# Sliding-window and chunked attention inside a two-block kernel: the division by the softmax sums moves from GpSimd to ScalarE, and two steps of VectorE move with it

## The chip, the cores and the metric

The kernel runs on one core of a Trainium2 chip. The metric is the device time in microseconds of one execution. Three executions of the kernel before took 1228.63, 1229.01 and 1231.67 us; the median is 1229.01 us.

## The reference

Two transformer blocks in fp32, one after the other, over 512 tokens of width 1024. The first block has a projection, sliding-window attention with sinks, a gated convolution, a merge, and a feed-forward part; the second is two layers, each with chunked attention under a relative bias and with retention.

```python
# first block: 8 heads of 64, blocks of 128 tokens, each sees itself and the one before
scores = einsum("bnqhgd,bnkhd->bnhgqk", q, kw) * 64 ** -0.5       # masked to a window of 128
probs = softmax(concatenate([scores, sink], axis=-1))[..., :-1]
out = einsum("bnhgqk,bnkhd->bnqhgd", probs, vw)
...
# second block, per layer: 8 heads of 64, causal by blocks, at most 8 chunks of 64 back
scores = einsum("bnqhd,bnkhd->bnhqk", qc, kb) * dh ** -0.5 + bias
p = softmax(where(valid, scores, NEG_INF))
out = einsum("bnhqk,bnkhd->bnqhd", p, vb)
```

## The kernel before

**Units.** The large products are cut into 196 units. A unit is one 128-column strip of a weight matrix against all 512 tokens: 8 steps of three matmuls (high part, low part and cross product of a split into two fp32r values). ScalarE makes the high part of a unit's weights (`w_hi`, L1104), VectorE the low part (`w_lo`, L1476), both for unit u+4 once unit u is done, so there are four sets of weights. When a unit is done VectorE takes its bank and multiplies by the norm's factor (`apply_factor`, L1513 and L1515). SyncE loads the raw weights in panels of two units (L553, L554). Each engine has its instructions in one fixed order, written out by hand, and waits on semaphores.

**Attention between the steps.** Attention is laid between the steps of these units in three places: in units 19 to 29 of the first projection ("attention 1"), and in units 11 to 23 of the projection of each of the second block's two layers ("layer 0", "layer 1"). The work is cut into rounds, two rounds to a pair. Attention 1 has 8 rounds (`ROUNDS1`), so 4 pairs; each layer has 10 rounds (`ROUNDS2`), so 5 pairs; 14 pairs in all. `ATT1_SLOTS` and `ATT2_SLOTS` hold the step numbers of slots. For slot r, with r even, and a pair of rounds r and r+1:

- At slot r TensorE makes the scores (`score`, L749), four slots later, 32 steps or 4 units, it mixes the values of that pair (`mix`, L736).
- VectorE scales, masks and takes the row peaks into `soft_pair` (`soften`, L1525, one buffer for each round of a pair, so the next pair's `soften` waits until this pair's is transposed).
- ScalarE takes the exponentials in place with their sums (`exps`, L1139).
- VectorE inverts the sums (`find_shares`, L1557), `SHARES_AFTER` = 5 steps after the slot, which puts it in the next unit.
- GpSimd multiplies each block of `soft_pair` in place by its share (`normalise`, L2093), 8 or 6 instructions to a pair.
- VectorE transposes within 32x32 blocks into `blocks_turned` (`turn`, L1571, four instructions to a pair), in slot r+1, which is 13 steps after slot r and opens the unit after that. There is one `blocks_turned`, so the first of them waits until the DMAs of the pair before have landed.
- SyncE moves the 32x32 blocks to their places with 16 DMAs (`move_blocks`, L537), queued between two panel loads (`moves_before`).
- TensorE's `mix` waits for all 16 to land; with two pairs in a row at one slot nothing else is interleaved.

In the second half of each layer's attention two more things are in the same queues: from unit 17 on ScalarE swaps the halves of a rotary tile (L1397, L1398), VectorE multiplies by the cosine (`rotate_straight`, L1937), GpSimd multiplies by the sine (L2119) and adds (L2126). ScalarE's swap stands behind `slot(2 * i)` of its unit, VectorE's multiplication ahead of the unit's `apply_factor`.

The buffers of a unit's result in these stretches are three banks in turn (`main_bank`), since the fourth serves the scores.

## Time and profile before

| | |
|---|---|
| median of three executions | 1229.01 us |
| the profiled execution | 1231.27 us |
| its span, first to last instruction | 1229.4 us |
| mean granted TensorE clock | 0.986 of full speed |
| attention 1 | about 119 to 205 us of the span |
| layer 0 | about 743 to 846 us |
| layer 1 | about 1018 to 1120 us |

The 1.9 us between the profiled execution's time and its span lie before the first and behind the last instruction of the program. A PE row is TensorE's matmul, PEld its weight load, DVE VectorE, ACT ScalarE, POOL GpSimd, SPq SyncE's issuing of DMAs. A time in brackets at the end of a row of a timeline is how long that engine sat idle before it, and behind the arrow stands what ended the wait.

### The profile page before, as it was taken

What the parts mean: (1) busy time and instruction counts of PE and PEld (TensorE: products, weight loads), DVE (VectorE), ACT (ScalarE), POOL (GpSimd) and SP (SyncE); (2) the same over time, 40 slices, a digit from 0 to 9 for tenths busy, and PEclk for the clock granted to TensorE, in tenths of its full rate; (3) what the DMA queues carried; (4) which work ended last, traced back from release to release, by engine and by line L of the source; (5) the groups of instructions that cost most, each with busy time, mean ns of one, the idle gap of its engine ahead of it and who ended that gap; (6) DMA issues with size and microseconds to landing.
All of it is one profiled execution on the core that took longest, in us unless ns stands there. A gap on an engine that the chain in (4) does not pass through costs nothing.

```text
span 1229.4 us, 15973 instructions
## 1 busy us (share of the span) xinstructions
PE 1189.4 (97%) x5752; PEld 979.5 (80%) x5752; DVE 724.6 (59%) x1237; ACT 501.9 (41%) x872; POOL 195.7 (16%) x175
## 2 busy tenths in 40 slices
PE   9999798999999999999999999889999999989998
PEld 8888677888888888888888887667888887767886
DVE  6555674474577777775642556666555336665554
ACT  5522441354443443442242424343654324434653
POOL 3000331001100000000010102484002003583000
PEclk9999998999999999999999999989999999999999
DMA  6323244223232233322223423543213423533221
GB/s 210 118 90 103 72 129 144 82 90 103 94 112 85 86 102 102 102 102 92 89 103 103 159 82 90 149 138 103 70 69 103 172 79 91 167 114 99 69 86 69
DMA packets 109131, 129.78 MB, mean 106 GB/s; under 512 B 7434, under 2 KB 86508, under 8 KB 108812
## 3 DMA queue, kind: packets, MB, share of 16 engines
q1 hardware_dynamic: 106539, 122.38, 31.2%
q10 hardware_dynamic: 2528, 6.56, 1.5%
q8 instruction: 39, 0.64, 0.2%
q14 instruction: 25, 0.20, 0.1%
HBM read 112.10 MB, written 2.14 MB: 93 GB/s over the span
## 4 chain that ended last, share of the span: by engine, by line
PE 77%; POOL 9%; DVE 5%; ACT 4%; issue 3%; SPq 2%; DMA 0%; DVEq 0%; ACTq 0%; POOLq 0%
PE main L669 18%; PE main L670 18%; PE main L671 18%; POOL soft_pair L2093 7%; PE aux L669 3%; PE aux L670 3%; PE aux L671 3%; PE main L995 2%; PE main L997 2%; PE main L996 2%; ACT soft_pair L1139 2%; SPq L537 2%; DVE soft_pair L1525 2%; ACT w_hi L1104 1%; PE aux L736 1%
## 5 line engine op out<-in xcount | busy, mean ns | idle before, releaser
L669 PE MATMUL main<-x_hi,w_hi 128*128 128x512 f32 x980 | 389.4, 397 | 0.0
L1476 DVE TENSOR_TENSOR w_lo<-raw,w_hi 128x1024 fp32r<-128x1024 f32 x192 | 245.7, 1281 | 239.1 <-ACT w_hi L1104 235.0
L670 PE MATMUL main<-x_lo,w_hi 128*128 128x512 f32 x980 | 382.4, 390 | 0.0
L671 PE MATMUL main<-x_hi,w_lo 128*128 128x512 f32 x980 | 382.0, 390 | 0.0
L1104 ACT ACTIVATE w_hi<-raw 128x1024 fp32r<-128x1024 f32 x192 | 202.0, 1056 | 273.9 <-PE main L671 173.4
L669 PEld LDWEIGHTS main<-x_hi,w_hi 128*128 128x128 f32 x980 | 184.7, 189 | 42.2 <-issue 5.5
L671 PEld LDWEIGHTS main<-x_hi,w_lo 128*128 128x128 f32 x980 | 184.3, 188 | 39.4
L670 PEld LDWEIGHTS main<-x_lo,w_hi 128*128 128x128 f32 x980 | 184.8, 189 | 36.3
L2093 POOL TENSOR_SCALAR soft_pair<-soft_pair,share 128x128 f32<-128x128 f32 (+2 forms) x96 | 103.8, 1099 | 288.3 <-DVE share L1557 288.3
L1139 ACT ACTIVATE soft_pair<-soft_pair,neg_peak 128x128 f32<-128x128 f32 (+2 forms) x96 | 50.2, 524 | 111.8 <-DVE neg_peak L1532 111.2
L2082 POOL COPY sum_sq<-squares 128x512 f32<-128x512 f32 x4 | 2.5, 613 | 467.1 <-ACT squares L1121 467.1
L1571 DVE STREAM_TRANSPOSE blocks_turned<-soft_pair 128x512 f32<-128x512 f32 (+1 forms) x56 | 37.6, 684 | 43.5 <-POOL soft_pair L2093 29.2
L2085 POOL TENSOR_TENSOR sum_sq<-sum_sq,squares 128x512 f32<-128x512 f32 x28 | 37.5, 1338 | 114.4 <-ACT squares L1121 113.8
L1513 DVE TENSOR_TENSOR up_in<-main,factor 128x512 f32<-128x512 f32 x44 | 30.4, 690 | 35.4 <-PE main L671 32.3
L995 PE MATMUL main<-w_hi,x_hi 128*128 128x512 f32 x128 | 50.5, 394 | 0.0
L997 PE MATMUL main<-w_lo,x_hi 128*128 128x512 f32 x128 | 50.0, 390 | 0.0
L996 PE MATMUL main<-w_hi,x_lo 128*128 128x512 f32 x128 | 49.9, 390 | 0.0
L1271 ACT ACTIVATE g_hi<-squares 128x512 f32 (+1 forms) x22 | 13.9, 633 | 66.0 <-DVE squares L1752 66.0
L669 PE MATMUL aux<-g_hi,w_hi 128*128 128x512 f32 x88 | 34.2, 389 | 0.0
L670 PE MATMUL aux<-g_lo,w_hi 128*128 128x512 f32 x88 | 34.2, 389 | 0.0
L671 PE MATMUL aux<-g_hi,w_lo 128*128 128x512 f32 x88 | 34.2, 389 | 0.0
L669 PE MATMUL main<-g_hi,w_hi 128*128 128x512 f32 x88 | 34.2, 389 | 0.0
(270 smaller groups left out, 1779.8 us busy)
## 6 DMA issues: line engine op xcount, KB each, us to landing
raw<-in_w_in_dram SPq DMA_DIRECT2D x96, 512.0 KB, 4.5
raw<-in_w_up_dram SPq DMA_DIRECT2D x44, 512.0 KB, 4.2
raw<-in_w_out_dram SPq DMA_DIRECT2D x24, 512.0 KB, 4.0
raw<-in_w_down_dram SPq DMA_DIRECT2D x22, 512.0 KB, 4.1
both_sums<-blocks_turned SPq DMA_DIRECT2D x96, 64.0 KB, 2.0
rel<-band_rows ACTq DMA_DIRECT2D x2, 2048.0 KB, 8.8
rel_part<-blocks_turned SPq DMA_DIRECT2D x64, 64.0 KB, 2.0
x_rows<-in_x_dram SPq DMA_DIRECT2D x4, 512.0 KB, 7.7
```

The costliest lines, as they stand in the source:

```text
L669: pe.matmul(bank, hi, right_hi[j], start=first and j == 0, stop=False)
L670: pe.matmul(bank, hi, right_lo[j], start=False, stop=False)
L671: done = pe.matmul(bank, lo, right_hi[j], start=False, stop=last and j == len(rows) - 1)
L995: pe.matmul(bank, x, hi, start=k == 0, stop=False)
L996: pe.matmul(bank, rest, hi, start=False, stop=False)
L997: return pe.matmul(bank, x, lo, start=False, stop=k == KT - 1)
L1104: act.activation(w_hi[:, u % 4, :, :], raw_unit(u), ACT.Copy).then_inc(hi_ready, 1)
L1139: done = act.activation(block, block, ACT.Exp, bias=neg_peak[which], accum_out=total[which])
L1476: dve.tensor_tensor(w_lo[:, u % 4, :, :], raw_unit(u), w_hi[:, u % 4, :, :].bitcast(F32), ALU.subtract).then_inc(lo_ready, 1)
L1571: dve.transpose(places.rearrange("p b (k i) -> p k b i", i=32), soft(r, half)[:, 0:width].rearrange("p (k b j) -> p k b j", b=4, j=32))\
L2085: pool.tensor_tensor(sum_sq[:, 0, :], sum_sq[:, 0, :], tile, ALU.add)\
L2093: done = pool.tensor_scalar(block, block, share[:, n % 2, half, step:step + 1], None, ALU.mult)
```

## The change

ScalarE multiplies by the shares, in place, with `activation(Copy, scale=share)`: for a pair of slot r in the unit of step slot + 8, ahead of that unit's weights. GpSimd does not take part in attention any more. The shares are found 4 steps behind the slot, which puts them in the slot's own unit, behind the exponentials and ahead of that unit's `apply_factor`. The odd slots move from 13 to 12 steps behind the even ones, and the transposes move from the opening of a unit to the unit before, behind its `apply_factor` and ahead of its `w_lo`. The points at which SyncE takes up the moves are written in other terms.

```diff
--- before.py
+++ after.py
@@ -69,9 +69,10 @@
 ROUNDS1 = [[(t, 2 * j), (t, 2 * j + 1)] for t in range(4) for j in range(2)]
 ROUNDS2 = [steps for t in (0, 2) for steps in
            ([(t, 0), (t, 2)], [(t, 3)], [(t + 1, 0), (t + 1, 2)], [(t, 1), (t + 1, 1)], [(t + 1, 3)])]
-ATT1_SLOTS = [156 + 16 * (r // 2) + 13 * (r % 2) for r in range(len(ROUNDS1) + 3)]
-ATT2_SLOTS = [92 + 16 * (r // 2) + 13 * (r % 2) for r in range(len(ROUNDS2) + 3)]
-SHARES_AFTER = 5
+ATT1_SLOTS = [156 + 16 * (r // 2) + 12 * (r % 2) for r in range(len(ROUNDS1) + 3)]
+ATT2_SLOTS = [92 + 16 * (r // 2) + 12 * (r % 2) for r in range(len(ROUNDS2) + 3)]
+SHARES_AFTER = 4
+DIVIDED_AFTER = 8
 
 STATES = NB - 1
 MIDDLE = SEQ // 2
@@ -522,9 +523,9 @@
     @block.sync
     def _(sp):
 
-        moves = [(ATT1_SLOTS[r + 1] / 8, r, turned1(r // 2)) for r in range(0, len(ROUNDS1), 2)]
+        moves = [((ATT1_SLOTS[r] + 16) / 8, r, turned1(r // 2)) for r in range(0, len(ROUNDS1), 2)]
         for layer in range(LAYERS):
-            moves += [(IN2 + LAYER_UNITS * layer + ATT2_SLOTS[r + 1] / 8,
+            moves += [(IN2 + LAYER_UNITS * layer + (ATT2_SLOTS[r] + 16) / 8,
                        len(ROUNDS1) + len(ROUNDS2) * layer + r, turned2(r // 2)) for r in range(0, len(ROUNDS2), 2)]
 
 
@@ -538,7 +539,7 @@
                         .then_inc(turned_ready[n // 2 % 2], 16)
 
         def moves_before(n):
-            while moves and moves[0][0] + 0.4 < 2 * n - 6:
+            while moves and moves[0][0] < 2 * n - 6:
                 unit, r, turned = moves.pop(0)
                 move_blocks(r, turned)
 
@@ -1144,6 +1145,14 @@
                 which = (slice(None), n % 2, slice(None), slice(0, len(spans)))
                 act.activation(sink_exp[which], sink_exp[which], ACT.Exp).then_inc(sinks_exp, 1)
 
+        def normalise(n, spans, pair):
+            act.wait_ge(shares_ready, n + 1)
+            for half in range(2):
+                for step, (t, b, blocks, columns) in enumerate(spans):
+                    block = pair[:, half, columns]
+                    done = act.activation(block, block, ACT.Copy, scale=share[:, n % 2, half, step:step + 1])
+                done.then_inc(probs_ready, 1)
+
         def attention_slot(r, first, rounds, soft, sinks):
             for m in rounds_scored(r, rounds):
                 exps(first + m, m, rounds[m], soft, sinks)
@@ -1201,6 +1210,10 @@
             for r, steps_before in enumerate(ATT1_SLOTS):
                 if 8 * u < steps_before <= 8 * u + 8:
                     slot1(r)
+            for r in range(0, len(ROUNDS1), 2):
+                if 8 * u < ATT1_SLOTS[r] + DIVIDED_AFTER <= 8 * u + 8:
+                    for m in (r, r + 1):
+                        normalise(m, rounds1[m], soft1_pair[m % 2])
             act.wait_ge(unit_done, u + 1)
             if u >= FIRST_UNITS:
                 split(u + 4)
@@ -1369,6 +1382,10 @@
                 for r, steps_before in enumerate(ATT2_SLOTS):
                     if 4 * s < steps_before <= 4 * s + 4:
                         slot2(r)
+                for r in range(0, len(ROUNDS2), 2):
+                    if 4 * s < ATT2_SLOTS[r] + DIVIDED_AFTER <= 4 * s + 4:
+                        for m in (r, r + 1):
+                            normalise(len(ROUNDS1) + len(ROUNDS2) * layer + m, rounds2[m], soft2_pair[m % 2])
                 if s >= 43:
                     ret_slot(s - 43)
 
@@ -1629,8 +1646,6 @@
 
 
         def slot1(r):
-            for m in rounds_turned(r, rounds1):
-                turn(m, m, rounds1[m], soft1)
             for m in rounds_scored(r, rounds1):
                 soften(m, m, rounds1[m], lambda t, b, half: window[:, 0 if b else P:256], 0.125,
                        lambda t, half: sink_cols[:, 2 * t + half:2 * t + half + 1], soft1)
@@ -1683,6 +1698,9 @@
                        cb[:, 0, :], cb[:, 1, :], cc[:, 0, :], cc[:, 1, :], cx[:, 0, :], cx[:, 1, :]]
             target = targets[u] if u < 12 else targets[u - 6] if u < 18 else gates[:, u - 18, :]
             apply_factor(u, target)
+            if 8 * u + 8 in ATT1_SLOTS:
+                for m in rounds_turned(ATT1_SLOTS.index(8 * u + 8), rounds1):
+                    turn(m, m, rounds1[m], soft1)
             if u >= FIRST_UNITS:
                 split(u + 4)
             if u in (11, 12, 17, 18):
@@ -1878,8 +1896,6 @@
                 first = len(ROUNDS1) + len(ROUNDS2) * layer
                 if r == 0:
                     dve.wait_ge(masked, layer + 1)
-                for m in rounds_turned(r, rounds2):
-                    turn(first + m, m, rounds2[m], soft2)
                 for m in rounds_scored(r, rounds2):
                     soften(first + m, m, rounds2[m],
                            lambda t, b, half: rel[:, 2 * t + half, (b + 1) * P - 1::-1], 1.0,
@@ -1984,6 +2000,9 @@
                     if i >= 28:
                         dve.wait_ge(y_ready, 8 * layer + i - 27)
                     apply_factor(u, gate2[:, u % 4, :])
+                if 8 * i + 8 in ATT2_SLOTS:
+                    for m in rounds_turned(ATT2_SLOTS.index(8 * i + 8), rounds2):
+                        turn(len(ROUNDS1) + len(ROUNDS2) * layer + m, m, rounds2[m], soft2)
                 if i < 31:
                     split(u + 4)
                 if i == 1:
@@ -2085,17 +2104,7 @@
                     pool.tensor_tensor(sum_sq[:, 0, :], sum_sq[:, 0, :], tile, ALU.add)\
                         .then_inc(sq_added, 1)
 
-        def normalise(n, r, spans, soft):
-            pool.wait_ge(shares_ready, n + 1)
-            for half in range(2):
-                for step, (t, b, blocks, columns) in enumerate(spans):
-                    block = soft(r, half)[:, columns]
-                    done = pool.tensor_scalar(block, block, share[:, n % 2, half, step:step + 1], None, ALU.mult)
-                done.then_inc(probs_ready, 1)
-
         gather(0, 0)
-        for r in range(len(ROUNDS1)):
-            normalise(r, r, rounds1[r], soft1)
         gather(KT, 1)
         pool.wait_ge(merged_ready, KT)
         pool.wait_ge(unit_done, UP)
@@ -2106,13 +2115,7 @@
 
 
             pool.memset(rel[0:64, :, 0:64], MASKED).then_inc(masked, 1)
-            first = len(ROUNDS1) + len(ROUNDS2) * layer
-            for r in range(6):
-                normalise(first + r, r, rounds2[r], soft2)
             for n in range(8 * layer, 8 * layer + 8):
-                if n % 8 in (1, 3):
-                    for r in (n % 8 + 5, n % 8 + 6):
-                        normalise(first + r, r, rounds2[r], soft2)
                 pool.wait_ge(swap_ready, n + 1)
                 if n == 0:
                     pool.wait_ge(rotary_ready, 2)
```

## Rows read from the trace of the kernel before

**Rows 1.** The page, busy time of the engines over the span.

```profile
PE 1189.4 (97%) x5752; PEld 979.5 (80%) x5752; DVE 724.6 (59%) x1237; ACT 501.9 (41%) x872; POOL 195.7 (16%) x175
```

**Rows 2.** The view of the tile blocks_turned: its instructions and who waited for it.

```profile
L537 SPq DMA_DIRECT2D both_sums<-blocks_turned x96: 507/591/1682, 141.4 to 1075.8; - x96
L1571 DVE STREAM_TRANSPOSE blocks_turned<-soft_pair x56: 535/711/718, 136.0 to 1103.2; 128x512 f32<-128x512 f32 x48, 128x384 f32<-128x384 f32 x8
...
  PEld aux L736: 39.5, 14
```

**Rows 3.** The timeline of PEld: two pairs' scores, then four pairs' mixing; last the idle time.

```profile
119.17 0.29 PEld L749 LDWEIGHTS aux<-k_twice,q 64*128 64x128 f32 x3 [0.42 <-issue]
...
132.05 0.19 PEld L749 LDWEIGHTS aux<-k_twice,q 64*128 64x128 f32 x2 [0.35 <-issue]
...
152.99 2.85 PEld L736 LDWEIGHTS aux<-both_sums,v_rows 128*64 128x64 f32 x28 [6.71 <-DMA both_sums<-blocks_turned]
...
202.70 1.51 PEld L736 LDWEIGHTS aux<-late_gates,v_rows 128*64 128x64 f32 x28 [0.75 <-DMA late_gates<-blocks_turned]
...
842.73 2.43 PEld L736 LDWEIGHTS aux<-rel_part,v 128*64 128x64 f32 x32 [2.71 <-DMA rel_part<-blocks_turned]
...
1116.55 3.15 PEld L736 LDWEIGHTS aux<-rel_part,v 128*64 128x64 f32 x32 [3.36 <-DMA rel_part<-blocks_turned]
```

**Rows 4.** Windows: length, busy PE, PEld, DVE, ACT, POOL, granted clock, DMA share, GB/s.

```profile
150.80:157.60 6.80, 4.61 (x31) 4.02 (x32) 3.55 (x6) 0.00 (x0) 6.04 (x7) 0.50 0.62 187
...
770.70:773.00 2.30, 0.67 (x6) 0.05 (x3) 0.05 (x1) 0.00 (x0) 2.30 (x3) 1.00 0.40 98
773.00:780.00 7.00, 7.00 (x54) 5.94 (x55) 5.05 (x17) 1.07 (x3) 3.88 (x5) 1.00 0.52 164
843.70:847.10 3.40, 3.40 (x26) 2.97 (x21) 0.62 (x2) 0.75 (x2) 0.00 (x0) 0.50 0.69 243
```

**Rows 5.** The chain that ended last, in attention 1: start, length, what.

```profile
133.53 7.12 POOL soft_pair L2093 x8
144.99 2.07 ACT soft_pair L1139 x8
...
149.74 7.11 POOL soft_pair L2093 x8
...
200.66 1.99 DMA late_gates<-blocks_turned
```

**Rows 6.** The timeline of SyncE's queue, first pair of attention 1.

```profile
141.42 10.11 SPq L537 DMA_DIRECT2D both_sums<-blocks_turned  x16
```

**Rows 7.** Groups by line and form: count, then busy us, mean ns of one.

```profile
L2093 POOL TENSOR_SCALAR soft_pair<-soft_pair,share 128x256 f32<-128x256 f32 x40 | 38.8, 985 | 0.0
...
L1139 ACT ACTIVATE soft_pair<-soft_pair,neg_peak 128x256 f32<-128x256 f32 x40 | 19.8, 496 | 21.5 <-DVE neg_peak L1532 21.4
...
L1139 ACT ACTIVATE soft_pair<-soft_pair,neg_peak 128x512 f32<-128x512 f32 x16 | 11.4, 713 | 39.7 <-DVE neg_peak L1532 39.7
...
L1139 ACT ACT_TABLE_LOAD x3 | 3.8, 1283 | 0.1
...
L1461 ACT ACTIVATE out_rows<-out_rows,r_tok 128x512 f32<-128x512 f32 x4 | 2.9, 723 | 0.1
```

**Rows 8.** The timeline of ScalarE and VectorE around the first pair.

```profile
130.84 1.99 ACT L1104 ACTIVATE w_hi<-raw 128x1024 fp32r<-128x1024 f32 x2
...
131.92 1.23 DVE L1476 TENSOR_TENSOR w_lo<-raw,w_hi 128x1024 fp32r<-128x1024 f32 x1 [2.20 <-ACT w_hi L1104]
```

**Rows 9.** The timeline of VectorE, unit 12 of layer 0.

```profile
752.78 0.69 DVE L1515 SCALAR_TENSOR_TENSOR q<-main,factor 128x512 f32<-128x512 f32 x1 [1.11 <-PE main L671]
```

**Rows 10.** The timeline of ScalarE, VectorE and GpSimd, fourth pair of layer 0.

```profile
798.25 0.63 ACT L1398 ACTIVATE swapped_pair<-straight_pair 64x512 f32<-64x512 f32 x1
...
798.91 0.69 DVE L1937 TENSOR_TENSOR straight_pair<-straight_pair,cos_t 128x512 f32<-128x512 f32 x1 [2.66 <-ACT swapped_pair L1398]
...
802.96 7.34 POOL L2093 TENSOR_SCALAR soft_pair<-soft_pair,share 128x512 f32<-128x512 f32 x6
```

## The prediction, made before the changed kernel ran

> **What bounds the kernel now.** I read the page first: TensorE is busy for 97% of the span [rows 1], so only time in which it stands still, or runs at the lower clock, can be won. Then the view of one tile, `blocks_turned`, through which every pair of attention goes: TensorE's weight loads waited 39.5 us for its DMAs, in 14 waits, one for each pair [rows 2]. The timeline shows them at the head of `mix`: 6.71 us before the first pair of attention 1, 0.75 before its fourth, 2.71 and 3.36 before the last pairs of the layers [rows 3]. Behind long waits comes a second loss: with the first the granted clock was 0.50, that is 1.2 GHz, from 150.8 to 157.6, and TensorE worked for 4.6 us of it; after a wait of 2.3 us it was still 1.00, or 2.4 GHz; at the end of layer 0 it was 0.50 again for 3.4 us, all of them busy [rows 4]. `mix` took 2.85 us at the lower clock and 1.51 at the higher [rows 3]. Half of the slow busy stretches is lost, but what lies ahead of a later wait of the same stage is swallowed by it; only what follows the last pair counts in full.
>
> The chain of waits says why the DMAs are late. In attention 1 it runs through GpSimd's division, 7.12 us for the first pair, then the last transpose, the next pair's `soften` and exponentials (to 147.06), and GpSimd again at 149.74; at the end it runs through the 16 issues and the last landing [rows 5]. That is a loop: the next pair can't be softened until this one is transposed, and it is 16.2 us long (149.74 less 133.53). TensorE's own distance between two slots with scores is 12.9 us (132.05 less 119.17 [rows 3]), 14.4 with a `mix` of 1.5 added, or 12.5 where no scores are left. So attention is too long a loop for the steps that cover it, and TensorE pays the difference at each `mix`. The end of each of the three stages is set by the last landing, so I compute when the last transposes end, pair by pair.
>
> **What the change removes: GpSimd's division.** One instruction of 256 columns takes 985 ns there. ScalarE's in-place instruction of that width takes 496 ns; its Copy with a scale of one value per partition takes 723 ns at 512 columns, where the exponential takes 713, so Copy with `share` costs like an exponential [rows 7]. A pair of attention 1 has eight: two of 128 columns at about 0.4 us, six at 0.5, together 3.8 instead of 7.12 us. A pair of the layers has six to eight, about 3.3. The 96 instructions put some 50 us on ScalarE, which is busy for 41% of the span [rows 1]; they are hidden behind TensorE's steps as long as the weights are ahead (below). A switch between Exp and Copy could cost a table load of 1283 ns, but the exponentials of 28 rounds, with `w_hi` copies between them, show three [rows 7]; I take none, and keep 14 x 1.3 us as the bad end.
>
> The Trainium skill (GPSIMD Engine Reference, section 4.1, Engine selection) says of GpSimd's elementwise work that "1-input is roughly line-rate". By that rule GpSimd would not be the slower engine, and the sum would lose the 3.3 us a pair that come from the engine. This case's rows, 985 against 496 ns, disagree with it.
>
> **What it moves: the shares.** The inverses stood behind a unit's product and `w_lo`; now VectorE waits for the exponentials in the slot's own unit. Queued behind that wait are the unit's product (0.7 us) and `w_lo`. For the first pair ScalarE is free at 130.84 and turns at once to `w_hi`; VectorE's `w_lo` of the same unit began at 131.92 [rows 8]. New order: shares to 131.4, product to 132.1, `w_lo` to 133.3, next product 133.9. ScalarE: `w_hi` to 131.9, then the eight divisions to 135.6; the following `w_hi` waits for them, where it had come at once. The first divided blocks are there at 132.8 and the last at 135.6, so VectorE's transposes follow its product from 134.2 (after a memset) nearly without a wait: four at 0.54 to 0.72 us [rows 2], last end 136.8. Before, the first issue was at 141.42 [rows 6]; 4.6 us are gained on the first pair, 3.3 of them by the engine and the rest by the order.
>
> **What sets the end then: the DMAs.** Sixteen issues take 10.11 us [rows 6], and from the first issue to the start of `mix` at 152.99 it is 11.6 [rows 3]. The least is 10.11 less 0.59 and plus the 1.99 us of the last landing [rows 5], 11.5; a single issue can take 1.68 us instead of 0.59 [rows 2], and with one such it is 12.6. I take 11.9, a little above the least, since most pairs show no long issue. `blocks_turned` is one buffer, so the next transposes wait for the landing, and the loop can't be shorter than 2.9 (transposes) + 11.9 = 14.8 us. VectorE's own loop is: `w_lo` 1.2, `soften` to the end of the exponentials 5.7 (147.06 less the end of transposing, 141.4), shares 0.4, product 0.7, `w_lo` 1.2, product 0.7, transposes 2.9, the rest of an attention output 0.7: 13.5. ScalarE fits within it. So the DMAs bound the loop, at 14.8 instead of 16.2 us.
>
> **Attention 1.** 136.8 + 3 x 14.8 + 11.9 = 193.1 for the last landing, against 202.70: 9.6 us gained. TensorE still waits: 2.4 us for the first pair (slot at 146.3), near 0 for the second, about 2 each for the third and fourth, whose slots hold no scores.
>
> **Layer 0.** The product that opens the transposes is the one at 752.78 [rows 9], so they end at 756.3. Two DMA loops: 785.9. From unit 17 on a longer chain holds in place of the DMAs, because ScalarE's division stands ahead of its rotary swap, and VectorE's cosine ahead of the product and the transposes: `w_lo` 1.2, `soften` and exponentials 5.2, swap 1.3 (twice 0.63 [rows 10]), `w_hi` 1.0, division 3.3, swap 1.3, cosine 0.7 [rows 10], product 0.7, transposes 2.9: 17.4 us, twice. The last transposes end at 820.7, the last landing is 832.6, against 842.73 [rows 3]: 10.1 gained. Before, GpSimd stood there with 7.34 us, and its own rotary work ahead of it [rows 10].
>
> **Layer 1.** The same stage; the last landing was 1116.55. It lacks 0.7 us of work on VectorE before the first pair, so it had less to gain: I take 8.9.
>
> **Clock.** 2.43 us for the last `mix` of layer 0 and 3.15 of layer 1 against 1.7 at the full clock, and 3.4 us at half speed behind each: up to 2.4 us a layer. A clock of 0.50 followed waits of 2.7 us and more [rows 3, 4], and waits of 2 to 4 us remain, so I take half, 2 us in all. Zero and 4.8 are the ends.
>
> **What costs nothing.** SyncE takes up each pair's moves ahead of the same panels as before: (156 + 16)/8 = 21.5 is below 22 as 21.525 was, and so on for all 14, and they end earlier, so the panels queued behind them come earlier. GpSimd's sine products are no longer behind a division, and can only come earlier. The cover for the later `w_hi` and `w_lo` is the lead of the weights: in my timeline `w_lo` of unit 24 ends at 138.0 and unit 24 starts at 153. Of the banks, the tightest is unit 19's product in layer 0 at 812, with unit 22 starting at 819. Without that cover each pair would pay its excess in full.
>
> **Sum.** 9.6 + 10.1 + 8.9 + 2 = 30.6 us off an execution of 1231.3 (span 1229.4 and 1.9 around it): 1200.7. The profiled execution is 2.3 above the median of the runs, 1229.0; measured like that median, 1198.5.
>
> **Rivals.** (a) *ScalarE's order costs more than I see.* The division waits for VectorE's shares with `w_hi` behind it, VectorE waits for `w_hi`, and the loop is 16 us, not 14.8. For it: the layers' chain of 17.4 shows that such orders bite. Against it: 1.3 us of slack in the loop above. Three loops at 1.2, four in the layers, and 2 more per swap chain: 3.6 + 4.8 + 2 = 10 less gained, 1208.5. Chance 0.2. (b) *More gained.* DMAs at 11.5 throughout give 0.4 on each of 14 pairs, and no clock drop gives 2.8 more: 1190. Chance 0.2. (c) *Slower.* The weights come late: in-order ScalarE holds `w_hi` behind a division that waits for shares, VectorE holds `w_lo` behind transposes that wait for a landing, and TensorE starves at a unit's start instead of at a `mix`. It decides only if these come over 7 us later than in my timeline (the bank of unit 22), and to end slower each of 14 pairs must then lose over 2.2 us more; at 2.6 each, 1235. Against it: the waits of the page are all for DMAs, none for weights. Chance 0.04. (d) *Nothing gained*: the change doesn't shorten what it means to, because ScalarE's division comes out as long as GpSimd's, 7.1 us a pair, and the loop stays at 16.2: 1229. The widths' durations speak against it [rows 7]. Chance 0.02. The rule of the Trainium skill quoted above would have this outcome. The forecast itself keeps 0.54.
>
> **Numbers.** 1198.5; 8 in 10 between 1189 and 1212: the lower end takes in most of (b), the upper one (a), and 3 us for longer issues. 0.3%, about what a measurement can tell here, is 3.7 us: faster 0.94, same 0.02, slower 0.04.
>
> **What would show it.** Right: ScalarE divisions of about 0.5 us for 256 columns, no extra table loads; first issue of the first pair near 136.8; starts of transposes 14.8 apart in attention 1, right behind a landing; waits for `blocks_turned` down from 39.5 to some 15 us, the largest before the last two pairs of a layer; last landing of attention 1 near 193, and of layer 0 10 us less after the start of its attention than before. Wrong: waits of TensorE on `w_lo` or on a product; divisions of over 0.7 us; transposes that start well after the landing; a clock at 0.50 for as long as before.

## The result and the profile after

The kernel after takes **1190.82 us** (median of 4 runs, 1190.60 to 1191.07); the kernel before, timed beside it, 1229.43 us (4 runs, 1228.63 to 1231.67). The ratio is 0.9683, with a 95% interval of 0.9666 to 0.9700: 38.6 us less. The forecast was 1198.5 us with a range of 1189 to 1212, so the direction and the range held, and the gain was 8 us larger than the 30.6 us of the sum (10 us larger between the two profiled executions, 1231.3 and 1190.6).

The page of the kernel after, busy time of the engines and the chain of waits:

```profile
PE 1177.2 (99%) x5752; PEld 968.9 (82%) x5752; DVE 712.5 (60%) x1237; ACT 543.2 (46%) x968; POOL 94.4 (8%) x79
...
PE 80%; SPq 8%; DVE 5%; issue 3%; ACT 3%; DMA 2%; DVEq 0%; POOL 0%; ACTq 0%; POOLq 0%
```

The chain of the kernel before, from its page:

```profile
PE 77%; POOL 9%; DVE 5%; ACT 4%; issue 3%; SPq 2%; DMA 0%; DVEq 0%; ACTq 0%; POOLq 0%
```

ScalarE took up 41 us of busy time (501.9 to 543.2 [rows 1]), GpSimd gave up 101. GpSimd's share of the chain fell from 9% to 0%, and SyncE's issuing rose from 2% to 8%; it is now the second member. The span is 1188.8 us.

The view of the tile `blocks_turned`:

```profile
L538 SPq DMA_DIRECT2D both_sums<-blocks_turned x96: 507/591/1340, 135.6 to 1042.9; - x96
L1588 DVE STREAM_TRANSPOSE blocks_turned<-soft_pair x56: 535/669/715, 133.4 to 1064.1; 128x512 f32<-128x512 f32 x48, 128x384 f32<-128x384 f32 x8
...
  PEld aux L737: 7.3, 7
```

TensorE's waits for the moved blocks fell from 39.5 us in 14 [rows 2] to 7.3 us in 7. Where they are, in the timeline of PEld (the four pairs of attention 1, the last pairs of the two layers; in brackets the wait):

```profile
147.41 1.51 PEld L737 LDWEIGHTS aux<-both_sums,v_rows 128*64 128x64 f32 x28 [1.81 <-DMA both_sums<-blocks_turned]
161.96 1.51 PEld L737 LDWEIGHTS aux<-late_gates,v_rows 128*64 128x64 f32 x28 [0.37 <-DMA late_gates<-blocks_turned]
176.62 1.51 PEld L737 LDWEIGHTS aux<-both_sums,v_rows 128*64 128x64 f32 x28 [2.21 <-DMA both_sums<-blocks_turned]
190.32 1.51 PEld L737 LDWEIGHTS aux<-late_gates,v_rows 128*64 128x64 f32 x28 [1.25 <-DMA late_gates<-blocks_turned]
...
817.16 1.73 PEld L737 LDWEIGHTS aux<-rel_part,v 128*64 128x64 f32 x32 [0.42 <-DMA rel_part<-blocks_turned]
...
1077.48 1.73 PEld L737 LDWEIGHTS aux<-rel_part,v 128*64 128x64 f32 x32 [0.57 <-DMA rel_part<-blocks_turned]
```

Against [rows 3], attention 1 ends 12.4 us earlier (202.70 to 190.32), layer 0 another 13.2 us after its own start (842.73 to 817.16 is 25.6, less the 12.4 it began earlier), layer 1 another 11.9 (39.1, less the 27.2 us by which it began earlier). 0.7 us of the 12.4 was there before attention began: its first scores are at 118.48, for 119.17 before. The rest of the 40.6 us of the two profiled spans, 3.1 us, follows behind the last pairs of the layers (1.6 and 1.5), where the clock no longer falls. The three stages of attention as windows of the kernel after (length, busy PE, PEld, DVE, ACT, POOL, granted clock, DMA share, GB/s):

```profile
119.00:205.00 86.00, 81.98 (x470) 66.27 (x467) 57.78 (x164) 44.29 (x122) 0.00 (x0) 1.00 0.43 123
729.00:830.00 101.00, 100.78 (x604) 80.11 (x603) 70.90 (x172) 59.10 (x138) 23.66 (x15) 1.00 0.44 128
1000.00:1090.00 90.00, 89.85 (x553) 72.19 (x552) 62.49 (x147) 51.60 (x119) 23.28 (x15) 1.00 0.50 141
```

No stretch of attention is at 0.50 now, and the wait of 2.21 us at 176.62 left the clock at 1.00, as one of 2.25 us did in the kernel before, at 772.97 [rows 4].

The first pair, in the timelines of VectorE and ScalarE:

```profile
130.57 0.18 DVE L1574 RECIPROCAL share<-total 128x4 f32<-128x4 f32 x1
130.66 0.66 DVE L1530 TENSOR_TENSOR gates<-main,factor 128x512 f32<-128x512 f32 x1
131.24 1.22 DVE L1493 TENSOR_TENSOR w_lo<-raw,w_hi 128x1024 fp32r<-128x1024 f32 x1
132.38 0.69 DVE L1530 TENSOR_TENSOR gates<-main,factor 128x512 f32<-128x512 f32 x1
133.06 0.27 DVE L1582 MEMSET blocks_turned<- 128x256 f32 x1
133.37 2.22 DVE L1588 STREAM_TRANSPOSE blocks_turned<-soft_pair 128x384 f32<-128x384 f32 x4
...
147.40 2.22 DVE L1588 STREAM_TRANSPOSE blocks_turned<-soft_pair 128x384 f32<-128x384 f32 x4 [2.08 <-DMA both_sums<-blocks_turned]
```

```profile
131.10 3.08 ACT L1153 ACTIVATE soft_pair<-soft_pair,share 128x128 f32<-128x128 f32 x8
134.08 1.04 ACT L1105 ACTIVATE w_hi<-raw 128x1024 fp32r<-128x1024 f32 x1
```

VectorE goes from the shares to the transposes without one wait. The next pair's transposes start at 147.40, when the last block of this one has landed: here the loop is bound by the moves.

### The profile page after: what moved, and what is told of

Its sections match the earlier page's. It is cut to its first block, busy times and chain, and to the rows that moved or that the text cites. A ratio compares the mean times of both kernels' runs of the same rounds, so it can differ in the third digit from the quotient of the medians.

```text
span 1188.8 us, 15973 instructions
## 1 busy us (share of the span) xinstructions
PE 1177.2 (99%) x5752; PEld 968.9 (82%) x5752; DVE 712.5 (60%) x1237; ACT 543.2 (46%) x968; POOL 94.4 (8%) x79
## 4 chain that ended last, share of the span: by engine, by line
PE 80%; SPq 8%; DVE 5%; issue 3%; ACT 3%; DMA 2%; DVEq 0%; POOL 0%; ACTq 0%; POOLq 0%
PE main L670 19%; PE main L671 19%; PE main L672 19%; SPq L538 8%; PE aux L670 3%; PE aux L671 3%; PE aux L672 3%; PE main L996 2%; PE main L998 2%; PE main L997 2%; DVE blocks_turned L1588 2%; DVE soft_pair L1542 1%; DMA both_sums<-blocks_turned 1%; ACT soft_pair L1140 1%; ACT soft_pair L1153 1%
## 5 line engine op out<-in xcount | busy, mean ns | idle before, releaser
L2122 POOL TENSOR_TENSOR swapped_pair<-swapped_pair,sin_t 128x512 f32<-128x512 f32 x16 | 26.8, 1674 | 241.8 <-ACT swapped_pair L1415 241.8
L1153 ACT ACTIVATE soft_pair<-soft_pair,share 128x128 f32<-128x128 f32 (+2 forms) x96 | 42.2, 521 | 0.0
L1588 DVE STREAM_TRANSPOSE blocks_turned<-soft_pair 128x512 f32<-128x512 f32 (+1 forms) x56 | 33.7, 660 | 9.8 <-DMA both_sums<-blocks_turned 6.9
L1280 ACT ACTIVATE gate_y<-gate_y 128x512 f32<-128x512 f32 x22 | 13.9, 634 | 45.4 <-DVE gate_y L1765 45.4
```

Source lines behind the costliest of these rows:

```text
L1153: done = act.activation(block, block, ACT.Copy, scale=share[:, n % 2, half, step:step + 1])
L1588: dve.transpose(places.rearrange("p b (k i) -> p k b i", i=32), soft(r, half)[:, 0:width].rearrange("p (k b j) -> p k b j", b=4, j=32))\
```

## The experiments

Theory A, the prediction's: the loop from one pair's transposes to the next was too long, and it got shorter by two things, a faster engine and a shorter order on VectorE; what is left is the time of SyncE's 16 moves. Rival B: the engine alone does it. Rival C: the order alone does it, and GpSimd could have stayed. A "loop" below is the time from the end of one pair's last transpose to the end of the next pair's; in attention 1 the kernel before had 16.2, 16.8 and 16.8 us. The kernels before each run are those timed on the same chip.

### The engine alone

ScalarE divides; slots, shares and transposes stay as before.

```diff
-ATT1_SLOTS = [156 + 16 * (r // 2) + 12 * (r % 2) for ...
+ATT1_SLOTS = [156 + 16 * (r // 2) + 13 * (r % 2) for ...   # ATT2_SLOTS alike
-SHARES_AFTER = 4
+SHARES_AFTER = 5
         def slot1(r):
+            for m in rounds_turned(r, rounds1):
+                turn(m, m, rounds1[m], soft1)               # slot2 alike
...
-            if 8 * u + 8 in ATT1_SLOTS:
-                for m in rounds_turned(ATT1_SLOTS.index(8 * u + 8), rounds1):
-                    turn(m, m, rounds1[m], soft1)
```

> ScalarE divides, but the shares are found in the next unit and the transposes open the unit after, as before the change. Theory (the loop from one pair's transposes to the next is a sum over engines in turn): ScalarE's division now stands ahead of w_hi, so VectorE's w_lo, which stands ahead of the transposes, comes after it: 5.7 to the end of the exponentials, w_hi 1.0, w_lo 1.2, shares 0.6, division 3.1, w_hi 1.0, w_lo 1.2, transposes 2.2, some 16.1 us a loop where the kernel before had 16.2. So nearly nothing is gained, 1220 to 1229 us. Rival (GpSimd's speed was the cost, the order is trimming): half or more of the 38.6 us, 1191 to 1210 us.

Measured: 1224.20 us, ratio 0.9956 (0.9940 to 0.9973). That is within the 1220 to 1229 us of theory A. In the old order a division of 3.09 instead of 7.12 us is worth some 5 us of 38.6. Rival B is out. The timeline of VectorE shows where the rest stays:

```profile
131.86 1.23 DVE L1493 TENSOR_TENSOR w_lo<-raw,w_hi 128x1024 fp32r<-128x1024 f32 x1 [2.20 <-ACT w_hi L1105]
...
137.48 1.23 DVE L1493 TENSOR_TENSOR w_lo<-raw,w_hi 128x1024 fp32r<-128x1024 f32 x1 [3.23 <-ACT w_hi L1105]
...
139.02 2.22 DVE L1588 STREAM_TRANSPOSE blocks_turned<-soft_pair 128x384 f32<-128x384 f32 x4
...
153.61 1.23 DVE L1493 TENSOR_TENSOR w_lo<-raw,w_hi 128x1024 fp32r<-128x1024 f32 x1 [3.21 <-ACT w_hi L1105]
```

ScalarE's divisions of the first pair end at 136.5, yet the transposes start at 139.0. VectorE stood still twice: 2.2 us in front of `w_lo` while ScalarE took exponentials and then `w_hi`, and 3.2 us in front of the next `w_lo`, because ScalarE's `w_hi` now stands behind the division. The shares and the transposes are queued behind these two. Two engines that wait for each other in turn add up their times: the loops were 15.7, 16.3 and 16.3 us, each only 0.5 us shorter than before, and TensorE waited 34.0 us in 13.

### The order alone

GpSimd divides with its code of before (behind `shares_ready`, pairs 4 and 5 of a layer between its rotary products); slots, shares and transposes as after.

```diff
-            for r in range(0, len(ROUNDS1), 2):             # on ScalarE
-                if 8 * u < ATT1_SLOTS[r] + DIVIDED_AFTER <= 8 * u + 8:
-                    for m in (r, r + 1):
-                        normalise(m, rounds1[m], soft1_pair[m % 2])
...
+        for r in range(len(ROUNDS1)):                       # on GpSimd
+            normalise(r, r, rounds1[r], soft1)
```

> The new order of shares and transposes, but GpSimd divides, at about 7.1 us a pair. Theory: loop w_lo 1.2, exponentials 5.7, shares 0.5, division 7.1, last transpose 0.7, 15.2 us instead of 16.2; with 2 us on each first pair some 4 to 6 us a stage, 1212 to 1217 us. Rival (the order is trimming): 1225 to 1229 us.

Measured: 1205.80 us, ratio 0.9809 (0.9793 to 0.9825), 22.7 us less than before. Theory A had missed here: it gave 1212 to 1217 us, with GpSimd's 7.1 us in full in a loop of 15.2. The loops of attention 1 are 13.8, 14.8 and 14.8 us, within 0.25 us those of the kernel after, and TensorE's waits 15.4 us in 8. GpSimd's timeline:

```profile
129.64 7.11 POOL L2104 TENSOR_SCALAR soft_pair<-soft_pair,share 128x128 f32<-128x128 f32 x8 [98.24 <-DVE share L1566]
143.02 7.09 POOL L2104 TENSOR_SCALAR soft_pair<-soft_pair,share 128x128 f32<-128x128 f32 x8 [6.28 <-DVE share L1566]
...
783.92 2.15 POOL L2137 TENSOR_TENSOR rq<-straight_pair,swapped_pair 128x512 f32<-128x512 f32 x1
786.06 7.13 POOL L2104 TENSOR_SCALAR soft_pair<-soft_pair,share 128x512 f32<-128x512 f32 x6
```

and VectorE's, in front of the transposes of these pairs:

```profile
136.78 0.71 DVE L1580 STREAM_TRANSPOSE blocks_turned<-soft_pair 128x512 f32<-128x512 f32 x1 [0.98 <-POOL soft_pair L2104]
...
149.09 2.22 DVE L1580 STREAM_TRANSPOSE blocks_turned<-soft_pair 128x384 f32<-128x384 f32 x4 [1.86 <-DMA both_sums<-blocks_turned]
...
788.16 0.71 DVE L1580 STREAM_TRANSPOSE blocks_turned<-soft_pair 128x512 f32<-128x512 f32 x1 [0.94 <-POOL soft_pair L2104]
```

In attention 1 the division of 7.1 us is nearly hidden, for three reasons. GpSimd starts at 129.64, on the first round, while ScalarE is still at the exponentials of the second, whose shares come 1.9 us later (131.53). The transposes follow it block by block. And from the second pair on the transposes can't start before the moves of the pair before have landed, at 149.09, when GpSimd has only 1.0 us of its division left (it ends at 150.11). The first pair's transposes end at 137.49, against 141.42 before [rows 6] and 135.59 after: the order took 3.9 us off the first pair, the engine 1.9 more at most (0.8 of it is that this execution reached the shares later, 131.53 against 130.75). What the engine gives lies in the second half of the layers, where GpSimd's own rotary products stand ahead of the division: for the fourth pair of layer 0 the shares were there at 780.95, the division began at 786.06, and VectorE waited at each transpose. TensorE also waited there for another product of VectorE's, `sum_sq` of the retention part, 1.5 us in layer 0 and 3.0 in layer 1, which it doesn't in the kernel after. Of the 17.4 us between this profiled span and that of the kernel after, 2.1 are there when attention 1 ends (0.8 of them when it begins), and 15.3 arise behind it.

Rival C is out as well: the order gives 22.7 us, and the engine, which gives 5 in the old order, gives another 15 in the new one (1205.8 to 1190.8). The two together give 38.6, some 10 more than the 22.7 and the 5 added up.

### The order cut in two

ScalarE divides; of the order's two parts one is taken over. With the shares early (transposes at the opening of the unit, 13 steps), against the kernel of the engine alone:

```diff
-SHARES_AFTER = 5
+SHARES_AFTER = 4
```

> ScalarE divides and the shares are found in the slot's own unit, but the transposes open the unit after, behind w_lo. Theory: loop 5.7 + w_hi 1.0 + division 3.1 + w_hi 1.0 + w_lo 1.2 + transposes 2.2 = 14.2 us, near the DMAs' loop of 14.1 to 14.5, and 3 to 4 us late on each stage's first pair: 1196 to 1206 us. Rival (the position of the transposes costs nothing once the engine is fast): 1190 to 1193 us.

With the transposes early (the shares in the next unit), against the kernel after:

```diff
-SHARES_AFTER = 4
+SHARES_AFTER = 5
```

> ScalarE divides and the transposes stand ahead of w_lo, but the shares are found in the next unit, behind w_lo. Theory: loop w_lo 1.5 + 5.7 + w_hi 1.0 + w_lo 1.2 + shares 0.6 + division 3.1 + last transpose 0.6 = 13.7 us, still under the DMAs' loop, so only the first pair of each stage is some 2 us later: 1192 to 1199 us. Rival (the shares' place is worth as much as the engine): 1205 us or more.

Measured: 1201.61 us (0.9775, 0.9759 to 0.9791) with the shares, within the 1196 to 1206 expected; 1201.02 us (0.9776, 0.9759 to 0.9792) with the transposes, where theory A had said 1192 to 1199 and missed; TensorE's waits 17.8 us in 9 and 12.0 us in 7. On top of the engine alone each part is worth some 23 us, both together 33: either breaks one of VectorE's two waits, and once the loop is near that of the moves the second has less left to win. With the early shares VectorE still waits 2.1 us in front of the `w_lo` ahead of the transposes; with the early transposes it still waits 2.2 us in front of the `w_lo` ahead of the shares. The two rows, one from each kernel:

```profile
136.00 1.23 DVE L1493 TENSOR_TENSOR w_lo<-raw,w_hi 128x1024 fp32r<-128x1024 f32 x1 [2.09 <-ACT w_hi L1105]
```

```profile
131.84 1.23 DVE L1493 TENSOR_TENSOR w_lo<-raw,w_hi 128x1024 fp32r<-128x1024 f32 x1 [2.20 <-ACT w_hi L1105]
```

In both the first pair of attention 1 is late enough for the clock to fall behind it. The kernel with the early transposes, in the timeline of PEld and in a window of 3.5 us:

```profile
149.02 1.82 PEld L737 LDWEIGHTS aux<-both_sums,v_rows 128*64 128x64 f32 x28 [2.82 <-DMA both_sums<-blocks_turned]
```

```profile
150.10:153.60 3.50, 3.50 (x20) 2.68 (x15) 3.50 (x10) 0.96 (x2) 0.00 (x0) 0.51 0.83 276
```

A wait of 2.82 us, and behind it 3.5 us of work at 1.2 GHz, half of which is lost. Attention 1 is still the smaller part of what these two kernels lack: it ends 4.1 us (early shares) and 1.4 us (early transposes) later than in the kernel after, and 0.8 and 0.6 of that were there when it began. The other 7.5 and 8.2 us of the profiled spans arise in the layers, where TensorE waits 1.6 to 2.3 us before each of the last two pairs, at full clock; with the early transposes it also waits 2.0 and 1.2 us for `sum_sq`.

### The swap ahead of the division

The prediction said that in the layers ScalarE's division, standing ahead of its rotary swap, makes a chain of 17.4 us. Here it stands behind.

```diff
                     act.activation(swapped(n)[64:128, :], straight(n)[0:64, :], ACT.Copy)
                         .then_inc(swap_ready, 1)
+                for r in range(0, len(ROUNDS2), 2):
+                    if 8 * i < ATT2_SLOTS[r] + DIVIDED_AFTER <= 8 * i + 4:
+                        for m in (r, r + 1):
+                            normalise(...)                  # and not ahead of the swap
```

> The changed kernel, with ScalarE's rotary swap of a unit ahead of the division (layers only). Theory (the order in ScalarE's queue sets the last two pairs of a layer): VectorE's cosine and product no longer wait for the division; the transposes of the fourth and fifth pairs of a layer begin about 2 us earlier, and TensorE's waits of 0.3 to 0.6 us there go; since they are short, 1 to 2 us in all, 1189 to 1190 us. Rival (TensorE no longer waits for anything there): 1190.8 us, unchanged within 0.3%, and the rows at mixing the same.

Measured: 1190.01 us, ratio 0.9676 (0.9662 to 0.9689), not to be told from the kernel after (0.9683). The waits before the last pairs are gone (0.35 us, issue alone), so the chain was real, but it only cost the 0.64 and 0.42 us that TensorE still waited there. The timeline of VectorE for the fourth and fifth pair of layer 0 also shows that the new order has a price:

```profile
782.45 1.78 DVE L1953 TENSOR_TENSOR straight_pair<-straight_pair,cos_t 128x512 f32<-128x512 f32 x1
...
785.37 2.49 DVE L1588 STREAM_TRANSPOSE blocks_turned<-soft_pair 128x512 f32<-128x512 f32 x4 [0.54 <-DMA both_sums<-blocks_turned]
...
800.47 2.49 DVE L1588 STREAM_TRANSPOSE blocks_turned<-soft_pair 128x512 f32<-128x512 f32 x4
```

The transposes start 0.9 and 2.1 us earlier than in the kernel after (786.27, 802.59), less than the 2.9 us of the division that left the swap's path: the cosine product now runs while GpSimd adds (781.52 to 783.68), and takes 1.78 us for 0.69. The loops there are 15.7 and 15.1 us instead of 16.4 and 16.3.

### Half of the moves on GpSimd's queue

What is left of theory A is that 16 issues on one queue set the loop where no swap chain does: in attention 1 and in the first two loops of a layer. GpSimd is idle in attention now, so it issues 8 of the 16, with a semaphore of its own for which `mix` and the next transposes also wait; first in attention 1 only, then in the layers as well.

```diff
+        def move_half(n, turned):                           # on GpSimd
+            pool.wait_ge(probs_turned, 2 * n + 4)
+            if n >= 4:
+                pool.wait_ge(mixed, n - 2)
+            for a in (2, 3):
+                for b in range(4):
+                    pool.dma_start(turned[32 * b:32 * b + 32, a, :], ...).then_inc(turned_too[...], 16)
...
-            for a in range(4):                              # on SyncE
+            for a in range(2):
                 for b in range(4):
                     sp.dma_start(turned[32 * b:32 * b + 32, a, :], ...)
```

> The changed kernel, with 8 of a pair's 16 moves issued by GpSimd in attention 1 (layers as they are). Theory (in attention 1 what is left is the loop through the 16 issues in a row, 14.3 us): issues take half, the landing comes 3 to 5 us earlier, the waits of 1.81, 0.37, 2.21 and 1.25 us at mixing go, 5 to 6 us less: 1185 to 1187 us. Rival (the landing is set by something else, or GpSimd's issues are slow): 1190 us or more, with the waits as they are or longer.

> The same in the layers too. Theory: TensorE's waits there are 2 us in all, so 1 to 2 us less than with attention 1 alone: 1183 to 1186 us; GpSimd's rotary work stands ahead of two pairs' moves and may cost that back. Rival (GpSimd's issues hold up the rotary work): slower than with attention 1 alone.

Measured: 1186.94 us (0.9646, 0.9633 to 0.9660) in attention 1 only, 1185.99 us (0.9640, 0.9627 to 0.9653) everywhere, both within what was expected (1185 to 1187, 1183 to 1186). The issuing queues of the first pair in the second kernel, SyncE's and GpSimd's, and TensorE's waits:

```profile
135.98 5.15 SPq L539 DMA_DIRECT2D both_sums<-blocks_turned  x8
```

```profile
136.26 4.09 POOL L2116 DMA_DIRECT2D both_sums<-blocks_turned  x8 [105.26 <-DVE blocks_turned L1591]
```

```profile
146.28 1.51 PEld L739 LDWEIGHTS aux<-both_sums,v_rows 128*64 128x64 f32 x28 [0.33 <-issue]
...
812.82 1.73 PEld L739 LDWEIGHTS aux<-rel_part,v 128*64 128x64 f32 x32 [0.35 <-issue]
```

The row of 10.3 us is 5.2 long, the loops of attention 1 are 11.9, 12.5 and 13.5 us where they were 14.0 to 14.7, and no `mix` waits for a landing. All that is left is `issue`, 0.33 to 0.76 us each. So in attention 1 the moves did set the loop of the kernel after. In the layers the last two loops stay at 16.4 and 16.3 us, those of the swap chain, and no `mix` is late for it. Only about 5 us were still behind the moves, and with no `mix` waiting for them a shorter loop has nothing more to win at these places.

### VectorE divides

If the loop on VectorE has slack, VectorE could divide, right ahead of its transposes and with no change of engine between. The order is that of after.

```diff
-            for r in range(0, len(ROUNDS1), 2): ...         # on ScalarE
+        def divide(n, r, spans, soft):                      # on VectorE, ahead of the transposes
+            dve.wait_ge(shares_ready, n + 1)
+            for half in range(2):
+                for step, (t, b, blocks, columns) in enumerate(spans):
+                    block = soft(r, half)[:, columns]
+                    done = dve.tensor_scalar(block, block, share[:, n % 2, half, step:step + 1], None, ALU.mult)
+                done.then_inc(probs_ready, 1)
```

> The changed kernel, but VectorE divides, right ahead of the transposes' wait, ScalarE doesn't. Theory (VectorE's own queue is near the bound): 8 instructions of about 0.25 us put 2 us on VectorE's loop, which was some 12.5 to 13.5 us beside 14.3 of the DMAs, so it becomes the bound in part: 1191 to 1197 us. Rival (any engine faster than GpSimd does as well, or better, since a hand-over between engines falls away): 1187 to 1191 us.

Measured: 1210.59 us, ratio 0.9843 (0.9830 to 0.9857), 20 us slower than the kernel after. Its timeline of VectorE, for the first pair of attention 1 and for the last two of layer 0:

```profile
133.21 2.05 DVE L1573 TENSOR_SCALAR soft_pair<-soft_pair,share 128x128 f32<-128x128 f32 x8
...
788.90 3.35 DVE L1573 TENSOR_SCALAR soft_pair<-soft_pair,share 128x512 f32<-128x512 f32 x6
...
807.18 4.48 DVE L1573 TENSOR_SCALAR soft_pair<-soft_pair,share 128x256 f32<-128x256 f32 x6
```

Both expectations missed: theory A had 1191 to 1197 us, its rival 1187 to 1191. The division itself is the shortest of the three engines', 2.05 us for the eight blocks against 3.08 on ScalarE and 7.1 on GpSimd. In attention 1 it does little harm. The first pair's transposes start at 135.57 instead of 133.37, the first `mix` waits 3.60 us and the clock falls, but the loops are 13.8, 14.4 and 14.4 us, no longer than in the kernel after, and attention 1 ends only 1.6 us later. The other 16.2 us of the two profiled spans' 17.8 arise behind it, in the layers. There the division stands in full in VectorE's part of the last two loops, beside GpSimd's rotary products, where it takes 3.35 and 4.48 us, and the cosine product ahead of it takes 1.78 us for 0.69; these loops are 18.4 and 19.4 us instead of 16.4 and 16.3. The Trainium skill (ScalarE: Activation LUTs, Rules for kernel authors) says for a multiplication "Use VectorE, not ScalarE"; the instructions of this case agree with it (2.05 against 3.08 us), the kernel does not.

### The swap and the halves together

> The kernel after, with both edits: ScalarE divides behind its rotary swap in the layers, and GpSimd's queue issues half of each pair's 16 moves. Theory (all that was left to win were waits of TensorE for a landing, and the halved moves alone took the last of them away): nothing is left for the other order, 1186, as with the halved moves alone, ratio 0.963 to 0.965. Rival (each edit keeps its own gain, since the swap's order frees VectorE earlier for something other than the moves): 0.8 us less, 1185.2.

> The halved moves alone once more, beside the combination on the same chip. Both theories: 1186, within 0.1% of what it took before; it is here so that a difference of 0.8 us can be read.

Both edits as above. Measured on one chip: 1185.77 us (0.9646, 0.9632 to 0.9659) for both, 1185.92 us (0.9645, 0.9632 to 0.9658) for the halves alone. The rival had the swap's order worth another 0.8 us; the difference is 0.15, within the spread of either. The swap's order adds nothing that can be told once no `mix` waits for its blocks.

## Why the prediction was right, and what of it was not

**The bound and the mechanism** were right, but not the engine's part in it. Attention was a loop over a pair that outran TensorE's steps; the change shortens it to that of the moves in attention 1 and to that of the swap chain late in the layers, and the halved moves and the swap's order show that these set it. What was wrong is the share of GpSimd's division: the run with the order alone has it and still has loops of 13.8 to 14.8 us in attention 1. TensorE's wait in front of `mix` was to fall from 39.5 to some 15 us; it fell to 7.3. In the summed gain attention 1 stood with 9.6, layer 0 with 10.1, layer 1 with 8.9 and the clock with 2; they were 12.4 (11.7 without the 0.7 us from ahead of it), 13.2, 11.9 and 3.1. Each of the first three was 2 to 3 us too small. All four erred to the same side, and so the result lay only 2 us above the lower end of the range.

**The division was mis-sized.** "Two of 128 columns at about 0.4 us, six at 0.5, together 3.8": the durations are right and their sum is not. The groups by line and form, and the time of the eight in a row above (3.08 us):

```profile
L1153 ACT ACTIVATE soft_pair<-soft_pair,share 128x256 f32<-128x256 f32 x40 | 17.1, 494 | 0.0
...
L1153 ACT ACTIVATE soft_pair<-soft_pair,share 128x128 f32<-128x128 f32 x24 | 9.3, 387 | 0.0
...
L1140 ACT ACT_TABLE_LOAD x3 | 3.8, 1283 | 0.1
```

Six of 494 and two of 387 ns are 3.74 us; the eight take 3.08. At seven passages from one to the next, 0.66 us less is 94 ns each by which the records overlap. The Trainium skill (ScalarE: Activation LUTs, What ACT_TABLE_LOAD costs) states it: "Back-to-back ACTIVATEs overlap by ≈ 93 ns." That line was not used. The other things said of ScalarE held: Copy with one scale per partition costs like an exponential (494 and 496 ns), and there is no table load more than before.

**The transposes were mis-sized** in the same way: 2.9 us for four, measured 2.22 in attention 1 and 2.48 in the layers. Durations of 535 to 715 ns were added up where the records overlap.

**The first pair.** The last transpose was forecast to end at 136.8; it ended at 135.59. This execution reached attention 0.7 us earlier than the one before did (`soften` at 124.43 against 125.12), and the rest is the two terms above. That "4.6 us are gained on the first pair, 3.3 of them by the engine and the rest by the order" has it the wrong way round: the order alone gave 3.9. The 3.3 us between the engines' divisions were for the most part not on the path, because GpSimd started on the first round while the second was still in its exponentials.

**The DMA loop** of 14.8 us was 14.0, 14.5 and 14.7 us in attention 1, and 14.9 and 14.0 in the first part of layer 0: shorter by the transposes. The moves themselves were sized right, 11.9 us, measured 11.8, 12.3, 12.4 and 11.5 from the last transpose to the landing. SyncE's queue for the first two pairs:

```profile
135.62 10.34 SPq L538 DMA_DIRECT2D both_sums<-blocks_turned  x16
...
149.65 10.88 SPq L538 DMA_DIRECT2D late_gates<-blocks_turned  x16
```

Eleven of the fourteen rows are longer than the 10.11 us of [rows 6]: "most pairs show no long issue" was too kind, and 11.9, chosen between 11.5 and 12.6, was right as a mean.

**Layer 0 and layer 1.** The swap chain of 17.4 us was there at 16.4 and 16.3. (Its terms as listed add up to 17.6, not 17.4; with that the gain of layer 0 would have been 9.7 us and not 10.1.) The last landing of layer 0 was to come 10.1 us earlier after the start of its attention; it came 13.2 earlier. In the order of the steps, 0.4 us came from the first pair, 0.7 from the two DMA loops, 2.1 from the two chains. With the chain at 16.3, TensorE's own steps nearly catch up: its waits before the last two pairs are 0.64 and 0.42 us, and not the 2 foreseen. Layer 1 was taken to gain 1.2 us less than layer 0, and gained 1.3 less (11.9 against 13.2).

**The clock.** Half of 4.8 us was taken, with 0 and 4.8 as ends. No clock fell in the kernel after, so the whole was won, but the whole was 3.1 us. The 4.8 counts one loss twice: the slow `mix` lies inside the stretch of 3.4 us at 1.2 GHz [rows 3, 4], and half of 3.4 us, in each of two layers, makes 3.4 in all. That 2 came close to 3.1 is luck, half of a term that was too large. That no clock fell hangs on the shorter loops: the largest wait that was left was 2.21 us, where the forecast had waits of 2 to 4.

**The rivals.** (b), more gained, 1190 us, is what came, but that its price fits is luck. Its 0.4 us on each of 14 pairs by moves of 11.5 us did not come (they were 11.5 to 12.4), and late in a layer the swap chain set the loop and not the moves; shorter divisions and transposes gave that gain instead. No fall of the clock came true, worth 1.1 us more than the 2 taken and not 2.8. (a), a dearer order on ScalarE, did not: VectorE has no wait for `w_hi` in the kernel after at the first pair, and the run with the engine alone shows what (a) looks like, loops of 16 us. (c), late weights, had no sign in any run. (d), nothing gained because the engine is no faster: GpSimd's instruction of 256 columns took 1049 ns in the run with the order alone and ScalarE's 494, so the rule "1-input is roughly line-rate" of the Trainium skill (GPSIMD Engine Reference, 4.1 Engine selection) is off by two here. (d)'s condition was false, so its price was not tested. It is doubtful all the same: GpSimd's own division in the new order, 7.1 us long, took 1205.8 us and not 1229. On ScalarE a division of that length would also have held up the `w_hi` behind it, and no run shows what that costs.

**What cost nothing** did so: the waits of TensorE in the kernel after hold none for the weights of a unit, and none for GpSimd's products but one of 1.0 us for `mean`, which the kernel before has too.

## What to carry to other kernels

Where two engines feed one another in turn (ScalarE's `w_hi`, VectorE's `w_lo`, then the shares, then the division, then the transposes), look first at what each is made to wait for by the queue's order, and only then at which engine is faster: here less than half the time for a step gave 5 us in the old order, and moving two steps past one wait each gave 23, with the slow engine kept. Then ask again: in the new order the same faster engine gave another 15, most of it where the slow one had other work in its queue. Once the order is right, the next bound is a row of small DMA issues on one queue, and an idle engine's queue takes half of it. And sum a row of equal instructions by the distance of their starts, not by their durations.

## What the runs showed of the hardware

- **GpSimd's issues are quicker than SyncE's for the same 64 KB moves**: 8 in 4.09 us against 8 in 5.15 us, side by side. With both queues at work a move lands 2.6 us (SyncE's) and 2.3 us (GpSimd's) after its issue in the median, where it had been 2.0, so they cost each other little.
- **VectorE and GpSimd share something.** `w_lo` of 1024 columns takes 1.18 to 1.23 us alone and 1.72 to 1.99 beside GpSimd's rotary products. The cosine product takes 0.69 us alone and 1.78 when it starts in the middle of one of GpSimd's. Where it starts first it is not slowed: in the kernel after one starts at 785.05 and takes 0.69, and GpSimd's sine product, which starts at 785.10, takes 1.79 where others take 1.3. None of the sixteen is slowed there, and the mean of the cosine product fell from 1187 to 687 ns with this change. The Trainium skill (SBUF — State Buffer, Who interferes with whom) has it: a VectorE instruction with two SBUF inputs contends with a GpSimd instruction that reads SBUF. The traces agree for these two. VectorE's division of six blocks, which has one SBUF tile as input, took 1.92 us alone and 3.35 and 4.48 us there.
- **The clock fell after waits shorter than the prediction had seen, and the length of the wait alone does not decide it.** TensorE's waits of 2.44 and 2.47 us (the engine alone, last pairs of the layers) were followed by 1.2 GHz, the second for 3.4 us (840.0 to 843.4), and so were 2.57 and 2.82. None of 2.34 us or less was. But neither was one of 2.77 us (the order alone, first pair), nor, in the kernel where VectorE divides, one of 2.75 us and one of 3.78; one of 3.82 in the same kernel was. The `mix` behind each of the last two shows it:

```profile
806.13 1.73 PEld L737 LDWEIGHTS aux<-rel_part,v 128*64 128x64 f32 x32 [3.78 <-DMA rel_part<-blocks_turned]
...
1075.11 3.28 PEld L737 LDWEIGHTS aux<-rel_part,v 128*64 128x64 f32 x32 [3.82 <-DMA rel_part<-blocks_turned]
```

What else decides is left open here.
